# Every fourth weight remainder of a down projection formed by an accumulating DMA within the SBUF

## The chip, the cores and the metric

The kernel runs on one core of one Trainium2 chip. The metric is the device time in microseconds (us) of one execution.

## What is computed

One layer of a diffusion backbone over 256 latent tokens of width 2048: a mixer (gated DeltaNet heads beside a convolution branch, with 256 context tokens) and then a SwiGLU feed-forward part. The change touches only the last product of the feed-forward part, the one with `w_down` (5632 x 2048, f32):

```python
def swiglu(h, w_gate, w_up, w_down):
    return (jax.nn.silu(h @ w_gate) * (h @ w_up)) @ w_down
...
hf = modulate(rms_norm(x, ffn_norm_pre[i]), sh2, sc2)
x = x + g2 * rms_norm(swiglu(hf, w_gate[i], w_up[i], w_down[i]), ffn_norm_post[i])
```

## The kernel before

**Products in three parts.** Each f32 operand is split into a value rounded to fp32r (`_hi`) and a remainder (`_lo` = f32 value minus `_hi`), and a product is the sum of three TensorE matmuls: hi by hi, hi by lo, lo by hi (`product` in the TensorE program, L1848).

**Units.** A weight is streamed in units of 128 partitions x 1024 f32 (512 KB). A unit passes through three tiles of four slots each (`RING = 4`, L47): SyncE loads it from HBM to `raw`; ScalarE copies `raw` to `w_hi` with rounding (L968, from `split`, L1295); VectorE subtracts, `w_lo = raw - w_hi` (L1376, from `split`, L1373); TensorE then runs 12 matmuls of 512 columns on it (two halves of 512 columns of the unit, two tiles of 128 tokens, three parts; `unit`, L2188). The gate and up projections take NG = 176 units, the down projection ND = 88 (v = 0 to 87, the loops at L793, L1325, L1799, L2229 and L2249).

**What orders the work.** Each engine runs its own program in order and waits on semaphores. For unit v of the down projection:

- SyncE issues the load of unit v into `raw` when both `w_hi` and `w_lo` of unit v - 4 have been written from the same slot (L795 and L796). It takes the units in order, so a wait for one unit also holds the loads of all later ones.
- ScalarE starts `w_hi` of unit v when the load has landed and when TensorE has finished unit v - 4, which frees the slots of `w_hi` and `w_lo` (L1296 and L1297). So a unit can be split at the earliest three units of TensorE time ahead of its use.
- VectorE forms `w_lo` when `w_hi` is there.
- TensorE waits for both semaphores `S["hi"]` and `S["lo"]`, which count units.

**Beside it.** From v = 8 to v = 54 two of every three units are accompanied by one 512 KB block of `w_mod` (32 in all, for the output gate): SyncE loads it to one of the four slots of `gin` behind the load of unit v + 1 (L807 to L812), and VectorE adds it to `macc` (L1816) behind the remainder of unit v. GpSimd's last work in the kernel is the load of `x` to `x1` before the feed-forward part (L963). At the end come the squares, the norm and eight stores of 256 KB (L1833 to L1840, L816).

**The last units.** The last four units are run token tile by token tile (L2249), and then the output is normed and stored.

The loop of SyncE:

```python
for v in range(ND):
    U = NG + v
    sp.wait_ge(S["hi"], B0 + U - RING + 1)
    sp.wait_ge(S["lo"], B0 + U - RING + 1)
    cc, g = divmod(v, FT // 2)
    sp.dma_start(raw[:, (R0 + U) % RING, :].rearrange("p (a b) -> p a b", a=2),
```

Of the kernel before, what the change touches and what calls it, by code (L numbers as in the profile page):

```python
# [21 lines left out]
F32 = mybir.dt.float32  # L22
F32R = mybir.dt.float32r
I32 = mybir.dt.int32
ALU = mybir.AluOpType
# [444 lines left out]
def layer(nc, x, cond, ctx, c_ctx, w_mod, b_mod, mix_norm_pre, mix_norm_post, w_in, qkv_conv, a_log, dt_bias,  # L470
# [9 lines left out]
    with es:  # L480
# [128 lines left out]
        def sem(name):  # L609
# [12 lines left out]
        f_mm, f_sg, f_an, f_tr, f_ah, f_al, f_sq, f_yg, f_rt, f_rc, f_out, f_end = (  # L622
            sem(f"f_{n}") for n in ("mm", "sg", "an", "tr", "ah", "al", "sq", "yg", "rt", "rc", "out", "end"))

        def need(eng, kind, *key):
            eng.wait_ge(S[kind], COUNT[kind, key])

# [106 lines left out]
        ND = 4 * (FT // 2)  # L734
        NG2 = 2 * KT
        GATE_AT = {8 + 3 * k // 2: k for k in range(NG2)}


        seq_h = {CTX: (hc_hi, hc_lo), LAT: (h_hi, h_lo), FFN: (h_hi, h_lo)}
# [4 lines left out]
        def _(sp):  # L744
# [48 lines left out]
            for v in range(ND):  # L793
                U = NG + v
                sp.wait_ge(S["hi"], B0 + U - RING + 1)  # L795
                sp.wait_ge(S["lo"], B0 + U - RING + 1)  # L796
                cc, g = divmod(v, FT // 2)
                sp.dma_start(raw[:, (R0 + U) % RING, :].rearrange("p (a b) -> p a b", a=2),
                             w_down_v[:, 2 * g:2 * g + 2, 512 * cc:512 * (cc + 1)]).then_inc(
                    landed[(R0 + U) % RING], 16)  # L800
                if v == 6:
                    need(sp, "yg", 1, 3)
                    sp.dma_start(gw_all[:, :], ffn_norm_post[0].partition_broadcast(P)).then_inc(small_in["c"], 16)
                    sp.wait_ge(S["zero"], 2)
                    sp.dma_start(macc[0:1, :], b_mod[0:1, 5 * D:6 * D]).then_inc(small_in["c"], 16)
                    sp.wait_ge(f_mm, NG)
                if v - 1 in GATE_AT:  # L807
                    k = GATE_AT[v - 1]
                    if k >= 4:
                        sp.wait_ge(g_acc, A0 + k - 3)  # L810
                    sp.dma_start(gin[:, k % 4, :],
                                 w_mod_v[:, k // 2, 5 * D + UN * (k % 2):5 * D + UN * (k % 2 + 1)]).then_inc(mod_in[k % 4], 16)  # L812
# [8 lines left out]
        def _(pool):  # L821
# [39 lines left out]
            for kind, key in PLAN:  # L861
# [46 lines left out]
                elif kind == "mk":  # L908
                    s, p, l = key
                    if l == 0:  # L910
                        need(pool, "kc", s, p)
                        need(pool, "lvl")
                    elif l == 1:
                        need(pool, "yone", s, p)
                    else:
                        need(pool, "z", s, p, l - 1)
                    pool.tensor_tensor(mkl[:, :, :, :].rearrange("p t h c -> p (t h) c"),  # L917
                                       kc[:, :, :, :].bitcast(F32).rearrange("p t h c -> p (t h) c"), bc(lvl[:, l, :], 1, 4),
                                       ALU.mult).then_inc(S[kind], 1)
                elif kind == "mlo":  # L920
                    s, p, t = key
                    need(pool, "z", s, p, LEVELS - 1)
                    need(pool, "mhi", s, p, t)
                    pool.tensor_tensor(mlo[:, t, :, :], mn[:, t, :, :], mhi[:, t, :, :].bitcast(F32),
                                       ALU.subtract).then_inc(S[kind], 1)
                elif kind == "vb":

                    s, p, i = key
                    par = PAIRS.index((s, p)) % 2
                    need(pool, "natc", "v", s, p)  # L930
                    need(pool, "bsig", s)
                    if (s, p, i) != (CTX, 0, 0):
                        prev = (s, p, i - 1) if i else (*PAIRS[PAIRS.index((s, p)) - 1], 1)
                        need(pool, "vn", *prev)
                        if i == 0 and prev[0] == LAT:
                            need(pool, "oT", prev[1])
                    for d in range(2):
                        ins = pool.tensor_tensor(rb[:, 2 * d:2 * d + 2, :], kvq["v"][:, par, tile_of(d, i), :, :],
                                                 bc(gates_[s]["beta"][:, d, tile_of(d, i), 2 * p:2 * p + 2], 2, P),
                                                 ALU.mult)  # L940
                    ins.then_inc(S[kind], 1)
                elif kind == "kd":

                    s, p, i = key
                    par = PAIRS.index((s, p)) % 2
                    need(pool, "kn", s, "k", p)
                    need(pool, "eall", s)
                    k = PAIRS.index((s, p))
                    if i:
                        need(pool, "st", s, p, 0)  # L950
                    elif k and PAIRS[k - 1][0] == CTX:
                        need(pool, "st", *PAIRS[k - 1], 1)
                    elif k:
                        need(pool, "mix_hi", p - 1)
                        need(pool, "mix_lo", p - 1)
                    for d in range(2):
                        ins = pool.tensor_tensor(kd[:, 2 * d:2 * d + 2, :], kvq["k"][:, par, tile_of(d, i), :, :],
                                                 bc(ex[s][:, 1, d, tile_of(d, i), 2 * p:2 * p + 2], 2, P), ALU.mult)
                    ins.then_inc(S[kind], 1)
                elif kind == "s2":  # L960

                    need(pool, "mix_lo", NP - 1)
                    pool.dma_start(x1[:, :, :], x_v).then_inc(x_again, 16)  # L963

        @block.scalar
        def _(act):
# [328 lines left out]
            def split(n, land, mm_done):  # L1295
                act.wait_ge(landed[(R0 + n) % RING], land)  # L1296
                act.wait_ge(f_mm, mm_done)  # L1297
                copy(w_hi[:, (B0 + n) % RING, :], raw[:, (R0 + n) % RING, :], "hi")
# [26 lines left out]
            for v in range(ND):  # L1325
                n = R0 + NG + v
                split(NG + v, 16 * (n // RING + 1), NG + v - RING + 1)
                if v == 4:
                    turned_hi(slice(4 * (FC - 1), 4 * FC), FC)
                if v == 8:  # L1330
# [16 lines left out]
        def _(dve):  # L1347
# [449 lines left out]
            with dve.Fori(2, FC) as c:  # L1797
                gate_up(c, False)
            for v in range(ND):  # L1799
                split(NG + v, B0 + NG + v + 1)  # L1800
                if v == 1:
                    product(FC, True)
                if v == 4:
# [40 lines left out]
        def _(pe):  # L1844
# [340 lines left out]
                    if t == NT - 1:  # L2185
                        ins.then_inc(f_mm, 1)

            def unit(slot, ready, k0, left, banks, first, last):  # L2188

                pe.wait_ge(S["hi"], ready)  # L2190
                pe.wait_ge(S["lo"], ready)
                for k in range(2):
                    col = slice(512 * k, 512 * (k + 1))
                    for t in range(NT):
# [34 lines left out]
            for v in range(ND - RING):  # L2229
# [4 lines left out]
                if v == 20:  # L2234
                    pe.wait_ge(f_al, 2 * FC)
                unit((B0 + NG + v) % RING, B0 + NG + v + 1, 2 * g, (act_hi, act_lo), 2 * cc, g == 0,
                     g == FT // 2 - 1)
                if v == 2:
                    turn(FC, True)
                if v in (57, 60):  # L2240
# [6 lines left out]
            for t in range(NT):  # L2247
                tok = slice(P * t, P * (t + 1))
                for v in range(ND - RING, ND):  # L2249
                    slot, k0 = (B0 + NG + v) % RING, 2 * (v % (FT // 2))  # L2250
                    if t == 0:
                        pe.wait_ge(S["hi"], B0 + NG + v + 1)
                        pe.wait_ge(S["lo"], B0 + NG + v + 1)
                    for k in range(2):
                        col = slice(512 * k, 512 * (k + 1))
                        ins = product(PS[:, 6 + t, :], (act_hi[:, k0 + k, tok], act_lo[:, k0 + k, tok]),
# [24 lines left out]
```

## Time and profile before

| | |
|---|---|
| median of 2 runs | 1625.05 us (1623.65 to 1626.45) |
| span of the profiled execution | 1622.9 us |
| TensorE busy | 1538.2 us, 95% of the span |
| VectorE busy | 1043.9 us, 64% |
| ScalarE busy | 769.2 us, 47% |
| GpSimd busy | 227.5 us, 14% |
| read from HBM | 331.15 MB, 205 GB/s over the span |

The profile is one execution on the chip; times in it are us unless marked ns. PE is TensorE, PEld its weight loads, DVE is VectorE, ACT is ScalarE, POOL is GpSimd, SP is SyncE. An engine with a "q" (SPq) is its queue of instructions, where the issues of DMAs appear. Lines (L1376) are lines of the kernel before. Matmuls are pipelined: their records overlap, so that the time of one matmul in a full stream is the distance between starts and not its duration.

### The profile page before, as it was taken

How to read it: one execution, taken by the hardware profiler on the slowest of the kernel's cores; microseconds unless marked ns; L12 is line 12 of the kernel's file. 1: busy time of each engine (PE TensorE's matmuls, PEld its weight loads, DVE VectorE, ACT ScalarE, POOL GpSimd, SP SyncE). 2: the span in 40 equal slices, each digit the busy share in tenths (PEclk: the TensorE clock that was granted, in tenths of full speed). 3: DMA queues.
4: the chain of work that ended last, by engine and by line, in shares of the span. 5: the costliest groups of instructions: out<-in, count | busy, mean ns of one | idle time of the engine just before them, and what ended most of it. 6: DMA issues, size and time to landing. Idle time of an engine off the chain costs nothing.

```text
span 1622.9 us, 25136 instructions
## 1 busy us (share of the span) xinstructions
PE 1538.2 (95%) x9297; PEld 1292.8 (80%) x9297; DVE 1043.9 (64%) x1458; ACT 769.2 (47%) x1045; POOL 227.5 (14%) x236
## 2 busy tenths in 40 slices
PE   4887999998999999999999999999999999999998
PEld 0557788887888898898877888888888888888786
DVE  1436899999896857675577544545454445777554
ACT  5536634444355745467356544444444443443432
POOL 2000223333332333244200000000000000000000
PEclk9998999999999999999999999999999999999999
DMA  9993555655564556554464666666666665998653
GB/s 353 400 378 108 180 186 194 197 178 184 173 202 134 174 199 191 174 196 134 139 231 132 207 185 192 188 188 191 185 192 194 184 191 187 334 325 319 223 187 135
DMA packets 190979, 334.59 MB, mean 206 GB/s; under 512 B 14707, under 2 KB 80355, under 8 KB 189986
## 3 DMA queue, kind: packets, MB, share of 16 engines
q1 hardware_dynamic: 190194, 330.89, 62.8%
q0 software_dynamic: 688, 2.39, 0.5%
q8 instruction: 63, 1.03, 0.2%
q14 instruction: 34, 0.27, 0.0%
HBM read 331.15 MB, written 2.10 MB: 205 GB/s over the span
## 4 chain that ended last, share of the span: by engine, by line
PE 81%; DVE 10%; DMA 2%; SPq 2%; ACT 2%; issue 2%; POOL 0%; DVEq 0%; ACTq 0%; POOLq 0%
PE PS L1848 66%; DVE cacc L1706 3%; DVE w_lo L1409 3%; DMA first<-in_w_mod_dram 2%; PE PS L1854 2%; PE PS L2117 2%; PE PS L2069 2%; PE PS L2163 2%; SPq L755 2%; DVE sil L1534 1%; PE PS L2015 1%; PE PS L1944 1%; PE PS L2059 1%; DVE xyi L1597 1%; DVE gh L1592 1%
## 5 line engine op out<-in xcount | busy, mean ns | idle before, releaser
L968 ACT ACTIVATE w_hi<-raw 128x1024 fp32r<-128x1024 f32 (+1 forms) x422 | 443.9, 1056 | 508.1 <-PE PS L1848 415.5
L1376 DVE TENSOR_TENSOR w_lo<-raw,w_hi 128x1024 fp32r<-128x1024 f32 x264 | 323.0, 1225 | 309.6 <-ACT w_hi L968 309.6
L1848 PE MATMUL PS<-w_hi,h_hi 128*128 128x512 f32 x704 | 275.7, 392 | 0.0
L1848 PE MATMUL PS<-w_hi,h_lo 128*128 128x512 f32 x704 | 274.6, 390 | 0.0
L1848 PE MATMUL PS<-w_lo,h_hi 128*128 128x512 f32 x704 | 274.4, 390 | 0.0
L1848 PE MATMUL PS<-h_hi,w_hi 128*128 128x256 f32 (+1 forms) x784 | 237.4, 303 | 0.0
L1409 DVE TENSOR_TENSOR w_lo<-raw,w_hi 128x1024 fp32r<-128x1024 f32 (+1 forms) x158 | 195.5, 1249 | 57.6 <-ACT w_hi L968 57.6
L1848 PE MATMUL PS<-h_hi,w_lo 128*128 128x256 f32 (+1 forms) x784 | 221.8, 283 | 0.0
L1848 PE MATMUL PS<-h_lo,w_hi 128*128 128x256 f32 (+1 forms) x784 | 221.6, 283 | 0.0
L1848 PEld LDWEIGHTS PS<-h_hi,w_hi 128*128 128x128 f32 (+1 forms) x784 | 148.5, 189 | 36.8 <-issue 30.2
L1848 PEld LDWEIGHTS PS<-w_hi,h_lo 128*128 128x128 f32 x704 | 132.4, 188 | 27.7
L1848 PEld LDWEIGHTS PS<-w_lo,h_hi 128*128 128x128 f32 x704 | 132.5, 188 | 27.1
L1848 PEld LDWEIGHTS PS<-w_hi,h_hi 128*128 128x128 f32 x704 | 132.5, 188 | 27.1 <-issue 0.2
L1848 PEld LDWEIGHTS PS<-h_lo,w_hi 128*128 128x128 f32 (+1 forms) x784 | 148.7, 190 | 0.7
L1848 PEld LDWEIGHTS PS<-h_hi,w_lo 128*128 128x128 f32 (+1 forms) x784 | 148.2, 189 | 0.1
L1848 PE MATMUL PS<-w_hi,act_hi 128*128 128x512 f32 x352 | 137.9, 392 | 0.0
L1848 PE MATMUL PS<-w_hi,act_lo 128*128 128x512 f32 x352 | 137.0, 389 | 0.0
L1848 PE MATMUL PS<-w_lo,act_hi 128*128 128x512 f32 x352 | 136.9, 389 | 0.0
L1706 DVE SCALAR_TENSOR_TENSOR cacc<-ub,vcol,cacc 128x196 f32<-128x196 f32 (+14 forms) x240 | 124.0, 576 | 0.2
L917 POOL TENSOR_TENSOR mkl<-kc,lvl 128x512 fp32r<-128x512 f32 x56 | 82.8, 1479 | 142.1 <-PE PS L2059 108.0
L1848 PE MATMUL PS<-hc_hi,w_hi 128*128 128x256 f32 (+1 forms) x272 | 82.5, 303 | 11.4 <-ACT w_hi L968 4.3
L1534 DVE SCALAR_TENSOR_TENSOR sil<-PS,vcol,sil 128x254 f32<-128x254 f32 (+1 forms) x160 | 76.7, 481 | 16.0 <-ACT sil L1095 10.1
(342 smaller groups left out, 2352.8 us busy)
## 6 DMA issues: line engine op xcount, KB each, us to landing
raw<-in_w_in_dram SPq DMA_DIRECT2D x128, 512.0 KB, 3.9
raw<-in_w_mod_dram SPq DMA_DIRECT2D x96, 512.0 KB, 4.9
raw<-in_w_gate_dram SPq DMA_DIRECT2D x88, 512.0 KB, 3.7
raw<-in_w_up_dram SPq DMA_DIRECT2D x88, 512.0 KB, 3.7
raw<-in_w_down_dram SPq DMA_DIRECT2D x88, 512.0 KB, 4.5
first<-in_w_mod_dram SPq DMA_DIRECT2D x64, 512.0 KB, 9.7
raw<-in_w_out_dram SPq DMA_DIRECT2D x32, 512.0 KB, 4.3
gin<-in_w_mod_dram SPq DMA_DIRECT2D x32, 512.0 KB, 5.9
```

The costliest lines, as they stand in the source:

```text
L755: sp.dma_start(first[:, slot, :].rearrange("p (a b) -> p a b", a=2), w_mod_v[:, 2 * j:2 * j + 2, part * D + q * 512:part * D + (q + 1) * 5 ...
L917: pool.tensor_tensor(mkl[:, :, :, :].rearrange("p t h c -> p (t h) c"), kc[:, :, :, :].bitcast(F32).rearrange("p t h c -> p (t h) c"), bc( ...
L968: act.activation(out_ap, in_ap, ACT.Copy).then_inc(S[kind], 1)
L1376: dve.tensor_tensor(w_lo[:, slot, :], raw[:, (R0 + n) % RING, :], w_hi[:, slot, :].bitcast(F32), ALU.subtract).then_inc(S["lo"], 1)
L1409: dve.tensor_tensor(lo, raw[:, at_ring[u] % RING, 0:sz], hi.bitcast(F32), ALU.subtract).then_inc(done, 1)
L1534: ins = dve.scalar_tensor_tensor(out=o, in0=pr[:, T * h + a + off:T * h + b + off], scalar=vcol[:, col:col + 1], in1=o, op0=ALU.mult, op1= ...
L1706: ins = dve.scalar_tensor_tensor(out=dst, in0=src, scalar=vcol[:, col:col + 1], in1=dst, op0=ALU.mult, op1=ALU.add)
L1848: ins = pe.matmul(out_ap, a[i], b[j], start=start and n == 0, stop=stop and n == 2, skip_group_check=grouped)
L1854: ins = pe.transpose(PS[:, bank_, P * n:P * (n + 1)], src, ident[:, :])
L2069: ins = pe.matmul(PS[:, b, P * n:P * (n + 1)], a, m, start=False, stop=True, skip_group_check=True)
L2117: ins = pe.matmul(PS[:, b, P * n:P * (n + 1)], a, m, start=True, stop=True)
L2163: ins = pe.matmul(PS[32 * tile:32 * tile + 1, 3, :], csil[:, LAT, j:j + 1], raw[:, n % RING, 512 * h:512 * (h + 1)], start=j == 0, stop=j ...
```

## The change

In the down projection the units v = 2, 6, 10, ..., 78 (`BY_DMA`, 20 units, all in the same slot of `raw` and `w_lo`) get their remainder in another way. ScalarE, after it has copied `raw` to `w_hi`, writes minus the same rounded value to `w_lo` (a second copy with scale -1). GpSimd waits for it and issues a DMA from `raw` to `w_lo`, both in the SBUF, that adds to what stands in `w_lo`: raw - w_hi. VectorE leaves these 20 units out. TensorE, and SyncE where it is to load the next unit into the slot of `raw`, wait for the DMA's semaphore in place of VectorE's; the counts of VectorE's semaphore go down by the units left out. The two semaphores are ones that the kernel already has (`S["masks"]` and that of the loads with "dt").

```diff
--- before.py
+++ after.py
@@ -622,6 +622,16 @@
         f_mm, f_sg, f_an, f_tr, f_ah, f_al, f_sq, f_yg, f_rt, f_rc, f_out, f_end = (
             sem(f"f_{n}") for n in ("mm", "sg", "an", "tr", "ah", "al", "sq", "yg", "rt", "rc", "out", "end"))
 
+        f_neg, f_sum = S["masks"], small_in["dt"]
+        NEG0, SUM0 = TOTALS["masks"], 16 * 3
+
+        def rest_ready(eng, v):
+
+            if v in BY_DMA:
+                eng.wait_ge(f_sum, SUM0 + 16 * (BY_DMA.index(v) + 1))
+            else:
+                eng.wait_ge(S["lo"], B0 + NG + v + 1 - sum(u < v for u in BY_DMA))
+
         def need(eng, kind, *key):
             eng.wait_ge(S[kind], COUNT[kind, key])
 
@@ -734,6 +744,7 @@
         ND = 4 * (FT // 2)
         NG2 = 2 * KT
         GATE_AT = {8 + 3 * k // 2: k for k in range(NG2)}
+        BY_DMA = [v for v in range(ND - 2 * RING) if v % 4 == 2]
 
 
         seq_h = {CTX: (hc_hi, hc_lo), LAT: (h_hi, h_lo), FFN: (h_hi, h_lo)}
@@ -793,7 +804,7 @@
             for v in range(ND):
                 U = NG + v
                 sp.wait_ge(S["hi"], B0 + U - RING + 1)
-                sp.wait_ge(S["lo"], B0 + U - RING + 1)
+                rest_ready(sp, v - RING)
                 cc, g = divmod(v, FT // 2)
                 sp.dma_start(raw[:, (R0 + U) % RING, :].rearrange("p (a b) -> p a b", a=2),
                              w_down_v[:, 2 * g:2 * g + 2, 512 * cc:512 * (cc + 1)]).then_inc(
@@ -961,6 +972,10 @@
 
                     need(pool, "mix_lo", NP - 1)
                     pool.dma_start(x1[:, :, :], x_v).then_inc(x_again, 16)
+            for n, v in enumerate(BY_DMA):
+                pool.wait_ge(f_neg, NEG0 + n + 1)
+                pool.dma_start(w_lo[:, (B0 + NG + v) % RING, :].bitcast(F32), raw[:, (R0 + NG + v) % RING, :],
+                               accum_op=ALU.add).then_inc(f_sum, 16)
 
         @block.scalar
         def _(act):
@@ -1325,6 +1340,9 @@
             for v in range(ND):
                 n = R0 + NG + v
                 split(NG + v, 16 * (n // RING + 1), NG + v - RING + 1)
+                if v in BY_DMA:
+                    act.activation(w_lo[:, (B0 + NG + v) % RING, :], raw[:, n % RING, :], ACT.Copy,
+                                   scale=-1.0).then_inc(f_neg, 1)
                 if v == 4:
                     turned_hi(slice(4 * (FC - 1), 4 * FC), FC)
                 if v == 8:
@@ -1797,7 +1815,8 @@
             with dve.Fori(2, FC) as c:
                 gate_up(c, False)
             for v in range(ND):
-                split(NG + v, B0 + NG + v + 1)
+                if v not in BY_DMA:
+                    split(NG + v, B0 + NG + v + 1)
                 if v == 1:
                     product(FC, True)
                 if v == 4:
@@ -2185,10 +2204,13 @@
                     if t == NT - 1:
                         ins.then_inc(f_mm, 1)
 
-            def unit(slot, ready, k0, left, banks, first, last):
+            def unit(slot, ready, k0, left, banks, first, last, v=None):
 
                 pe.wait_ge(S["hi"], ready)
-                pe.wait_ge(S["lo"], ready)
+                if v is None:
+                    pe.wait_ge(S["lo"], ready)
+                else:
+                    rest_ready(pe, v)
                 for k in range(2):
                     col = slice(512 * k, 512 * (k + 1))
                     for t in range(NT):
@@ -2234,7 +2256,7 @@
                 if v == 20:
                     pe.wait_ge(f_al, 2 * FC)
                 unit((B0 + NG + v) % RING, B0 + NG + v + 1, 2 * g, (act_hi, act_lo), 2 * cc, g == 0,
-                     g == FT // 2 - 1)
+                     g == FT // 2 - 1, v)
                 if v == 2:
                     turn(FC, True)
                 if v in (57, 60):
@@ -2250,7 +2272,7 @@
                     slot, k0 = (B0 + NG + v) % RING, 2 * (v % (FT // 2))
                     if t == 0:
                         pe.wait_ge(S["hi"], B0 + NG + v + 1)
-                        pe.wait_ge(S["lo"], B0 + NG + v + 1)
+                        rest_ready(pe, v)
                     for k in range(2):
                         col = slice(512 * k, 512 * (k + 1))
                         ins = product(PS[:, 6 + t, :], (act_hi[:, k0 + k, tok], act_lo[:, k0 + k, tok]),
```

## Rows read from the trace of the kernel before

**Rows 1.** Page, chain that ended last: shares of the span, by engine.

```profile
PE 81%; DVE 10%; DMA 2%; SPq 2%; ACT 2%; issue 2%; POOL 0%; DVEq 0%; ACTq 0%; POOLq 0%
```

**Rows 2.** Chain in order of time, 1340 to 1623 us: start, us, what (first and last pieces).

```profile
1344.56 35.41 PE PS L1848 x156
1379.97 0.87 PE PS L1854 x8
1380.84 149.62 PE PS L1848 x660
...
1542.10 73.50 PE PS L1848 x324
...
1618.62 1.32 DVE x L1840 x2
```

**Rows 3.** Waits, 1360 to 1612 us: who waited for whom, us, times, longest.

```profile
ACT w_hi L968 <- PE PS L1848: 139.4, 84, 3.4
DVE w_lo L1376 <- ACT w_hi L968: 79.2, 80, 2.1
...
ACT w_hi L968 <- DMA raw<-in_w_down_dram: 1.7, 2, 1.5
```

**Rows 4.** Timeline of ACT: start, us, operation [idle before <-releaser].

```profile
1381.85 2.96 ACT L968 ACTIVATE w_hi<-raw 128x1024 fp32r<-128x1024 f32 x3
...
1405.44 1.06 ACT L968 ACTIVATE w_hi<-raw 128x1024 fp32r<-128x1024 f32 x1 [1.66 <-PE PS L1848]
1408.16 1.06 ACT L968 ACTIVATE w_hi<-raw 128x1024 fp32r<-128x1024 f32 x1 [1.66 <-PE PS L1848]
```

**Rows 5.** Timeline of DVE, the same stretch.

```profile
1406.53 1.23 DVE L1376 TENSOR_TENSOR w_lo<-raw,w_hi 128x1024 fp32r<-128x1024 f32 x1 [0.30 <-ACT w_hi L968]
1407.67 1.28 DVE L1816 SCALAR_TENSOR_TENSOR macc<-gin,csil,macc 128x1024 f32<-128x1024 f32 x1
```

**Rows 6.** Timeline of SP, the same stretch.

```profile
1405.53 0.46 SPq L811 DMA_DIRECT2D gin<-in_w_mod_dram  x1
1407.83 0.37 SPq L798 DMA_DIRECT2D raw<-in_w_down_dram  x1
1408.25 0.46 SPq L811 DMA_DIRECT2D gin<-in_w_mod_dram  x1
```

**Rows 7.** Line L798, loads of the down units, and stretches of the DMA view.

```profile
DMA to landing us min/median/max: 3.5/4.5/7.6
...
raw<-in_w_down_dram SPq DMA_DIRECT2D x37, 512.0 KB, 5.0
gin<-in_w_mod_dram SPq DMA_DIRECT2D x25, 512.0 KB, 5.8
...
raw<-in_w_down_dram SPq DMA_DIRECT2D x24, 512.0 KB, 3.6
```

**Rows 8.** Windows: us, PE, PEld, DVE, ACT, POOL busy (count), PEclk, DMA share, GB/s.

```profile
20.00:40.00 20.00, 12.36 (x68) 3.15 (x68) 5.46 (x30) 18.41 (x22) 0.00 (x0) 1.00 1.04 409
60.00:80.00 20.00, 18.01 (x148) 11.67 (x148) 8.38 (x18) 8.89 (x14) 0.00 (x0) 1.00 1.06 402
120.00:140.00 20.00, 13.35 (x82) 11.50 (x81) 11.66 (x28) 9.69 (x18) 0.00 (x0) 0.79 0.45 134
...
1400.00:1500.00 100.00, 100.00 (x443) 82.84 (x442) 74.59 (x62) 40.41 (x41) 0.00 (x0) 1.00 0.92 326
1560.00:1600.00 40.00, 40.00 (x178) 33.13 (x177) 19.26 (x17) 16.63 (x19) 0.00 (x0) 1.00 0.60 195
```

**Rows 9.** GpSimd: its last DMA (timeline), and that DMA from issue to landing.

```profile
821.04 0.78 POOL L963 DMA_DIRECT2D x<-in_x_dram x1 [28.41 <-DVE hc_lo L1678]
...
x<-in_x_dram POOLq DMA_DIRECT2D x1, 2048.0 KB, 9.0
```

## The prediction

> **What bounds the kernel now.** I began with the page's chain that ended last: 81% of it is TensorE, 10% VectorE [rows 1]. The chain in order of time says where: from 1344.56 us to the end of the matmuls at 1615.6 it is TensorE alone, matmul behind matmul, and only about 7 us of norm and store behind it [rows 2]. The whole down projection lies in that stretch. The stretch rows agree: TensorE is busy 100.00 of 100 us at a granted clock of 1.00, while VectorE has 74.59 and ScalarE 40.41 [rows 8]. Then I read who waits. TensorE waits for nobody in this stretch; ScalarE waits 139.4 us in 84 waits for TensorE, since it may write a slot only when the unit four back is done, and VectorE waits for ScalarE [rows 3]. So the splits run as early as the slots let them, and the work of VectorE is off the path.
>
> **The clock of the pipeline.** Two successive copies of ScalarE start at 1405.44 and 1408.16 [rows 4]: a unit of TensorE takes 2.72 us (12 matmuls), four units, one turn of the ring, take 10.88. The down projection is 88 x 2.72 = 239 us. A copy starts right when TensorE has done the unit four back, so TensorE wants the unit 3 x 2.72 = 8.16 us after the start of its copy. Today both parts are there after 2.3 us (copy 1405.44, remainder 1406.53 with 1.23 us [rows 4, 5]), some 5.9 us early; the next load into the same slot is issued then (1407.83 [rows 6]), lands 3.6 us later where there are no gate loads and 5.0 where there are [rows 7], and waits 3 to 5 us more for its copy.
>
> **What is removed.** 20 remainders of VectorE at 1.23 us, 24.6 us of busy time [rows 5]. Worth 0: it lies beside TensorE, which waits for none of it [rows 2, 3]. Where a remainder is left out the next `macc` step may start 1.2 us earlier, which nobody waits for either.
>
> **What is added, cheap parts.** 20 copies of ScalarE with scale -1. I take the price of a copy in a row: three took 2.96 us against 1.06 for one, so 0.95 each, 19 us in all [rows 4]. ScalarE is busy 40% of the stretch [rows 8], so its time is hidden too; behind it waits only the copy of the next unit, 2.72 - 2.01 = 0.7 us later, which isn't delayed. GpSimd has nothing else in this stretch (0.00 busy [rows 8]), so its wait holds nobody; its issue took 0.78 us at the last load of x [rows 9], against SyncE's 0.37 [rows 6].
>
> **The DMA itself.** No row shows an accumulating DMA or one inside the SBUF, so I bound X, the time from ScalarE's negated copy to the semaphore. A plain 512 KB load lands in 3.5 us at best [rows 7]. At the rate of a full queue, 402 GB/s [rows 8], its 0.524 MB take 1.30 us, so 2.2 us are fixed. From below: a plain load plus the slower issue, 3.5 + 0.4 = 3.9. From above: GpSimd's own 2048 KB load, four times the bytes in one direction, 9.0 us [rows 9]. I take the value near the lower end, because the size is the same and only the traffic is more: source and old contents are both read, so two streams, 2.2 + 0.4 + 2 x 1.30 = 5.2 us. With three streams in turn (the write apart too) it would be 6.5. The Trainium skill (Collectives: The Full Stack, The bandwidth ceiling) says that an add in the DMA's stream halves the rate, because it takes two source reads; no row here shows that, and by it X would be the same 5.2. The skill's fit for a DMA issued from GpSimd (DMA: Bandwidth & Descriptors, Anatomy of one DMA), about 2.0 us plus the bytes at 436 GB/s, makes 3.2 us for a plain one, below my lower end; its load of 2 MB would take 6.8, where the trace has 9.0 beside other loads. By that fit rival A below would hold.
>
> **For TensorE's own wait:** 1.06 + 0.95 + 5.2 = 7.2 us, under the 8.16 that there are. Taken alone, the remainder is in time, with 1 us in hand.
>
> **For the slot of `raw` it is another sum.** All 20 units use one slot, so the next load into it starts only after the DMA, and the loads behind it on SyncE's queue, of `raw` and of `gin`, are held with it. The turn of this slot is: copy and negated copy 2.0, DMA X, landing L, and 0.3 for three handoffs of about 0.1 each (my allowance, from copy ends and remainder starts some 0.1 apart [rows 4, 5]). It must not be over 10.88. With X = 5.2 there are 3.4 us for L; in the quiet stretch L is 3.6 to 3.7 [rows 7], so the turn takes 11.2, 0.3 too long. Eight turns lie there (v = 2 and 54 to 78): 8 x 0.3 = 3 us.
>
> **In the stretch of the gate loads** the engines are nearly full: 0.92 share, 326 GB/s [rows 8], 62 transfers in 100 us [rows 7], 6.75 per turn. These are 6.75 x 1.30 = 8.8 us of DMA time out of 10.88. The accumulation adds 2.6, 11.4 us, more than a turn already. On top, SyncE's queue is held until the sum has landed, so that it runs dry: nothing moves in the fixed part of the next load, 2.2 us. The turn becomes 8.8 + 2.6 + 2.2 = 13.6, 2.7 too long; the slot's own turn with L = 5.0 would be 12.5, so the DMA time is what binds. Sums of v = 6 to 50 hold loads in this stretch: 12 turns, 12 x 2.7 = 33 us. The Trainium skill (DMA: Bandwidth & Descriptors, Issuing engines are not separate DMA queues) says the same against this change: a DMA of GpSimd runs on the same 16 engines and interleaves with SyncE's. Were the GpSimd queue separate, this stretch would cost only 12 x 1.6 = 19 us.
>
> **Sum.** 3 + 33 = 36 us on the path, nothing taken from it: 1622.9 + 36 = 1659 for the profiled execution. The median of the runs is 2 us above the span, so 1661; I say 1660.
>
> **The rivals.** (A) The DMA is hidden: X at 3.9 or less, running while older loads still fill the engines, so that the dry 2.2 us don't arise. Then DMA time is 8.8 + 1.3 = 10.1 per turn, under 10.88, and the quiet turn is 2.3 + 3.9 + 3.7 = 9.9. Cost 0 to 10 us, 1623 to 1635. For it: the slack of 5.9 us at the unit and 3 to 5 us at the load. Against it: 0.92 share in 12 of 20 turns [rows 8]. The point that decides is X of about 4 us. (B) The forecast, X from 3.9 with the dry time (12.3 per turn, 12 x 1.4 = 17 us, 1642) to 6.5 (14.9, 12 x 4.0 + 8 x 1.6 = 61 us, 1686). (C) The add itself is slow, so that X is 7 to 9 or more. At 9.0 a quiet turn is 15.0 and the other one 8.8 + 6.4 + 2.2 = 17.4: 8 x 4.1 + 12 x 6.5 = 111 us, 1736; by the slot's turn alone (16.3) 98 us, 1723. TensorE then also waits for the sum itself, since 2.0 + 9 is over 8.16. For it: nothing in the trace prices the add. (D) Faster: the freed 24.6 us of VectorE would have to be on the path somewhere. The place would be a `macc` step late for a remainder; but VectorE waits for ScalarE before nearly all of its remainders (80 waits [rows 3]), so I give it next to nothing; its price is below 5 us. (E) TensorE's clock. The waits of TensorE come back each turn, some 2.7 us long. In one window with TensorE busy 13.35 of 20 us the clock is 0.79, between its levels of 2.4 and 1.2 GHz, and in one with 12.36 it is 1.00 [rows 8], so such gaps may but needn't lower it. A unit at 1.2 GHz takes 2.72 us more: 20 of them, 54 us on top, 1714. The Trainium skill (TensorE: Matmul & The Clock Gate, HAM oscillation) warns of this case, matmuls that start slow behind every wait for a DMA.
>
> **How the numbers follow.** A 0.27, B 0.43, C 0.25, D 0.02, E 0.03. 2% (about what a measurement can tell from no change) is 32.5 us, or 1657.5: 1.6 us per turn over all 20. B straddles it: its lower third, 0.13, counts as no change. Faster by over 2%: 0.02 at most. Within: 0.27 + 0.13 = 0.40. Slower: 0.30 + 0.25 + 0.03 = 0.58. The range goes from A's lower end, 1623, to 1730, inside C, which leaves out some 0.15. B's own range is 1642 to 1686.
>
> **What would show it.** GpSimd's 20 DMAs with a median landing near 5.2 us (3.9 for A, 7 and more for C). TensorE with new waits in the down projection: about 2.7 us each, 12 of them, in the stretch of the gate loads, and next to none later. ScalarE waiting for the loads of every fourth unit in place of TensorE. SyncE waiting for the sum before the loads of v = 6, 10, ... A GB/s in the gate stretch that is lower than 326. VectorE 24 us less busy, ScalarE 19 more. I am wrong if X is well off 5.2, or if the loads behind the held one catch up without the dry time.

## The result

The changed kernel takes 1681.76 us (median of 2 runs, 1679.35 to 1684.16) against 1625.05: 1.034 times the time before, 95% interval 1.032 to 1.036, or 57 us slower. Its profiled execution has a span of 1682.4 us against 1622.9. Times here are medians of the fast runs; two far slower ones (8672 us in the run with TensorE's `w_lo` matmuls last, 3097 us in the one with every fifth unit) are left out.

### The profile after

The page, part 1: busy time of each engine. It answers the table of before.

```profile
PE 1557.2 (93%) x9297; PEld 1304.3 (78%) x9297; DVE 1020.0 (61%) x1438; ACT 787.6 (47%) x1065; POOL 244.6 (15%) x256
```

VectorE is relieved by 23.9 us, ScalarE has 18.4 more, and none of the relief is in the time. The chain of the page, part 4, shows what took the place of TensorE's 81% [rows 1]:

```profile
PE 72%; DMA 11%; DVE 9%; ACT 4%; issue 2%; SPq 2%; POOL 0%; DVEq 0%; ACTq 0%; POOLq 0%
PE PS L1867 57%; DMA w_lo<-raw 5%; DMA raw<-in_w_down_dram 3%; DVE w_lo L1427 2%; DVE cacc L1724 2%; DMA first<-in_w_mod_dram 2%; PE PS L1873 2%; PE PS L2088 2%; PE PS L2136 2%; PE PS L2182 2%; ACT w_hi L983 1%; SPq L766 1%; PE PS L2034 1%; DVE sil L1552 1%; PE PS L1963 1%
```

The sum itself and the load of a weight now stand on the path. (The "sum" is from here on the accumulating DMA.) TensorE runs the same 9297 matmuls and is busy 19.0 us longer, 1557.2 against 1538.2, and it waits 41.3 us for sums, as the waits below show; together these are about the 59.5 us that the span grew. Lines of the changed kernel: L977 is the sum's DMA, L1344 the negated copy, L983 the copy to `w_hi`, L1867 a matmul, L809 a load, L631 and L633 the waits for a sum and for VectorE.

Windows of the changed kernel (us, busy time of PE, PEld, DVE, ACT, POOL, clock, DMA share, GB/s); before, TensorE was busy 100.00 of 100 us in the stretch of the gate loads [rows 8]:

```profile
1450.00:1470.00 20.00, 17.01 (x68) 13.35 (x66) 10.75 (x9) 6.33 (x7) 0.84 (x1) 0.91 0.87 272
1470.00:1490.00 20.00, 13.22 (x54) 10.49 (x54) 8.76 (x8) 7.28 (x10) 0.83 (x1) 0.90 0.72 221
...
1590.00:1616.00 26.00, 26.00 (x109) 20.12 (x108) 11.14 (x12) 10.90 (x11) 1.69 (x2) 1.00 0.71 209
1616.00:1640.00 24.00, 24.00 (x108) 19.87 (x107) 11.00 (x11) 11.95 (x15) 1.69 (x2) 1.00 0.83 246
```

Only the stretch with gate loads is damaged. Behind it TensorE is full again, with a sum in every turn there too. The timeline of GpSimd gives the length of the turns (start, us, instruction):

```profile
1387.63 0.86 POOL L977 DMA_DIRECT2D w_lo<-raw  x1 [12.70 <-ACT w_lo L1344]
...
1570.60 0.84 POOL L977 DMA_DIRECT2D w_lo<-raw  x1 [12.62 <-ACT w_lo L1344]
...
1620.52 0.84 POOL L977 DMA_DIRECT2D w_lo<-raw  x1 [10.06 <-ACT w_lo L1344]
1631.45 0.85 POOL L977 DMA_DIRECT2D w_lo<-raw  x1 [10.09 <-ACT w_lo L1344]
```

From v = 6 to v = 54 there are twelve turns in 183.0 us: 15.25 each, 4.4 over the 10.88 of before, 52 us of the 59.5 that the span grew. The last turn shown, in the quiet stretch behind the gate loads, is 10.93.

Why the two differ is in the landing times (the DMA view of the changed kernel, 1400 to 1500 us, and then 1610 to 1650 us: count, size, median us from issue to landing):

```profile
raw<-in_w_down_dram SPq DMA_DIRECT2D x24, 512.0 KB, 7.3
gin<-in_w_mod_dram SPq DMA_DIRECT2D x17, 512.0 KB, 8.1
w_lo<-raw POOLq DMA_DIRECT2D x7, 512.0 KB, 8.1
...
raw<-in_w_down_dram SPq DMA_DIRECT2D x15, 512.0 KB, 5.0
w_lo<-raw POOLq DMA_DIRECT2D x4, 512.0 KB, 4.4
```

The same sum takes 4.4 us in the quiet stretch and 8.1 beside the gate loads; the loads went from 5.0 and 5.8 [rows 7] to 7.3 and 8.1. Who waits for it (waits of the changed kernel, 1360 to 1672 us, and the same for SP):

```profile
DVE macc L1835 <- DMA gin<-in_w_mod_dram: 87.7, 27, 7.3
ACT w_hi L983 <- DMA raw<-in_w_down_dram: 80.1, 30, 7.7
...
PE PS L1867 <- DMA w_lo<-raw: 41.3, 13, 5.3
...
SPq L631 <- DMA w_lo<-raw: 197.9, 20, 12.6
```

And the chain in order of time shows two loops that take turns (start, us, what):

```profile
1418.39 7.29 DMA w_lo<-raw
1425.70 0.02 SPq L631
1425.72 0.03 issue
1425.75 4.47 DMA raw<-in_w_down_dram
1430.21 0.02 issue
1430.24 1.06 ACT w_hi L983
1431.30 0.95 ACT w_lo L1344
1432.25 0.28 issue
1432.54 8.95 DMA w_lo<-raw
1441.49 0.14 issue
1441.62 4.60 PE PS L1867 x12
...
1446.30 1.06 ACT w_hi L983
```

Loop one: sum, load of `raw` that was held for it, two copies, next sum. Loop two: sum, TensorE's unit that waited for it (4.6 us here and not 2.7), two copies, next sum. Both begin with the sum, and both are some 15 to 16 us long when the sum takes 8 to 9.

What such a sum meets is in the DMA view of its own time. During the one of 1403.80 us the queue of the loads moves 1.53 MB beside the sum's 0.52. All of it together flows at some 400 GB/s in the first 3.2 us, with the loads that had been held for the sum before, and at under 130 in the last 2.

### The profile page after: what moved, and what is told of

It is laid out like the page before. It is cut to its first block, busy times and chain, and to the rows that moved or that the text cites. A ratio compares the mean times of both kernels' runs of the same rounds, so it can differ in the third digit from the quotient of the medians.

```text
span 1682.4 us, 25156 instructions
## 1 busy us (share of the span) xinstructions
PE 1557.2 (93%) x9297; PEld 1304.3 (78%) x9297; DVE 1020.0 (61%) x1438; ACT 787.6 (47%) x1065; POOL 244.6 (15%) x256
## 4 chain that ended last, share of the span: by engine, by line
PE 72%; DMA 11%; DVE 9%; ACT 4%; issue 2%; SPq 2%; POOL 0%; DVEq 0%; ACTq 0%; POOLq 0%
PE PS L1867 57%; DMA w_lo<-raw 5%; DMA raw<-in_w_down_dram 3%; DVE w_lo L1427 2%; DVE cacc L1724 2%; DMA first<-in_w_mod_dram 2%; PE PS L1873 2%; PE PS L2088 2%; PE PS L2136 2%; PE PS L2182 2%; ACT w_hi L983 1%; SPq L766 1%; PE PS L2034 1%; DVE sil L1552 1%; PE PS L1963 1%
## 5 line engine op out<-in xcount | busy, mean ns | idle before, releaser
L983 ACT ACTIVATE w_hi<-raw 128x1024 fp32r<-128x1024 f32 (+1 forms) x422 | 443.7, 1056 | 541.6 <-PE PS L1867 376.6
L1394 DVE TENSOR_TENSOR w_lo<-raw,w_hi 128x1024 fp32r<-128x1024 f32 x244 | 298.4, 1225 | 303.1 <-ACT w_hi L983 303.0
L1867 PE MATMUL PS<-w_hi,h_hi 128*128 128x512 f32 x704 | 275.6, 392 | 0.0
L1867 PE MATMUL PS<-w_hi,h_lo 128*128 128x512 f32 x704 | 274.5, 390 | 0.0
L1867 PE MATMUL PS<-w_lo,h_hi 128*128 128x512 f32 x704 | 274.4, 390 | 0.0
L1867 PE MATMUL PS<-h_hi,w_hi 128*128 128x256 f32 (+1 forms) x784 | 237.7, 303 | 0.0
L1867 PE MATMUL PS<-h_hi,w_lo 128*128 128x256 f32 (+1 forms) x784 | 221.9, 283 | 0.0
L1867 PE MATMUL PS<-h_lo,w_hi 128*128 128x256 f32 (+1 forms) x784 | 221.8, 283 | 0.0
L1867 PE MATMUL PS<-w_hi,act_hi 128*128 128x512 f32 x352 | 144.5, 411 | 41.3 <-DMA w_lo<-raw 41.3
L1867 PEld LDWEIGHTS PS<-h_hi,w_hi 128*128 128x128 f32 (+1 forms) x784 | 148.8, 190 | 36.7 <-issue 31.8
L1867 PEld LDWEIGHTS PS<-w_hi,h_lo 128*128 128x128 f32 x704 | 132.4, 188 | 27.8
L1867 PEld LDWEIGHTS PS<-w_hi,h_hi 128*128 128x128 f32 x704 | 132.4, 188 | 27.3 <-issue 0.2
L1867 PEld LDWEIGHTS PS<-w_lo,h_hi 128*128 128x128 f32 x704 | 132.5, 188 | 26.9
L1867 PEld LDWEIGHTS PS<-h_lo,w_hi 128*128 128x128 f32 (+1 forms) x784 | 149.0, 190 | 0.7
L1867 PEld LDWEIGHTS PS<-h_hi,w_lo 128*128 128x128 f32 (+1 forms) x784 | 148.5, 189 | 0.1
L1867 PE MATMUL PS<-w_lo,act_hi 128*128 128x512 f32 x352 | 141.9, 403 | 0.0
L1867 PE MATMUL PS<-w_hi,act_lo 128*128 128x512 f32 x352 | 141.3, 401 | 0.0
L977 POOL DMA_DIRECT2D w_lo<-raw x20 | 17.0, 848 | 802.7 <-ACT w_lo L1344 802.7
L1867 PEld LDWEIGHTS PS<-w_hi,act_hi 128*128 128x128 f32 x352 | 68.8, 196 | 61.3 <-issue 46.9
```

The source lines that it names most:

```text
L977: pool.dma_start(w_lo[:, (B0 + NG + v) % RING, :].bitcast(F32), raw[:, (R0 + NG + v) % RING, :], accum_op=ALU.add).then_inc(f_sum, 16)
L983: act.activation(out_ap, in_ap, ACT.Copy).then_inc(S[kind], 1)
L1394: dve.tensor_tensor(w_lo[:, slot, :], raw[:, (R0 + n) % RING, :], w_hi[:, slot, :].bitcast(F32), ALU.subtract).then_inc(S["lo"], 1)
L1867: ins = pe.matmul(out_ap, a[i], b[j], start=start and n == 0, stop=stop and n == 2, skip_group_check=grouped)
```

## The experiments

Each edit is against the changed kernel unless said. The runs of the kernel before on the same chips lay at 1625.8 to 1626.7 us.

### Where the sum stands

```diff
-        BY_DMA = [v for v in range(ND - 2 * RING) if v % 4 == 2]
+        BY_DMA = [v for v in range(54, ND - 2 * RING) if v % 4 == 2]
```

> Only the seven sums of v = 54 to 78 are left, those behind the gate loads; every other remainder is VectorE's again. Theory (the price of a sum is its sharing of the DMA engines with the gate loads, which makes it land after 7 to 9 us in place of 4.3): hardly any cost, 1625 to 1631 us, the sums land in about 4.3 us. Rival (each sum costs the same wherever it stands, 57 us / 20 = 2.8 us): 7 x 2.8 = 20 us, 1645 us.

Measured 1626.03 us, ratio 1.0004 (0.9994 to 1.0014): seven sums for nothing. They landed in 4.4 us (min/median/max of the line of the sum), and TensorE stayed full, as the window shows:

```profile
DMA to landing us min/median/max: 4.3/4.4/4.5
...
1500.00:1560.00 60.00, 60.00 (x259) 48.31 (x258) 30.15 (x29) 26.88 (x29) 3.47 (x4) 1.00 0.77 239
```

An equal price per sum is refuted. Nor is there a gain: VectorE's work was free.

Then the gate loads were taken away instead:

```diff
-                    if k >= 4:
-                        sp.wait_ge(g_acc, A0 + k - 3)
-                    sp.dma_start(gin[:, k % 4, :],
+                    if k < 4:
+                        sp.dma_start(gin[:, k % 4, :],
...
-                    dve.wait_ge(mod_in[k % 4], 16 * (2 * NMOD // NF + k // 4 + 1))
+                    if k < 4:
+                        dve.wait_ge(mod_in[k % 4], 16 * (2 * NMOD // NF + k // 4 + 1))
```

> The changed kernel with only the first four of the 32 gate loads; the later steps of macc read these four again and wait for no load (so the output gate is wrong). All 20 sums are left. To be held against the kernel before with the same omission. Theory (sharing with the gate loads is the price): the sums land in 4.3 to 5 us, the cost over its control is under 12 us: 1625 to 1637 us. Rival (the slot's turn is too long anyway, or the sum is dear by itself): the cost stays above 30 us, over 1655 us.

The same edit to the kernel before:

> The control: the kernel before with the same omission of 28 gate loads. TensorE waits for nothing in the down projection before, so both theories expect no gain: 1622 to 1626 us.

Measured 1638.70 us and 1625.58 us: the cost of 20 sums falls from 57 to 13.1 us. The theory had said under 12, so it is a near miss. The chain in order of time and the times of the sums tell where most of the 13 are. The sums of v = 6 and 10 still run in the stretch of the four gate loads and the 1 MB load of `gw_all`, and take 8.56 and 7.84 us; their two turns are 16.0 and 14.5 us long, 8.7 us too long together. From the fourth on the turns are 11.15 in the mean (v = 14 to 54), and the chain looks like this:

```profile
1472.19 0.96 ACT w_lo L1343
1473.15 0.28 issue
1473.43 4.48 DMA w_lo<-raw
...
1477.97 4.58 DMA raw<-in_w_down_dram
1482.55 0.02 issue
1482.57 1.06 ACT w_hi L982
```

This is the turn of the slot: sum, load, two copies and the handoffs, 4.5 + 4.6 + 2.0 + 0.3 + 0.1 = 11.4 us as rounded here, where 10.88 would be free.

### What the add costs

```diff
-                pool.dma_start(w_lo[:, (B0 + NG + v) % RING, :].bitcast(F32), raw[:, (R0 + NG + v) % RING, :],
-                               accum_op=ALU.add).then_inc(f_sum, 16)
+                pool.dma_start(w_lo[:, (B0 + NG + v) % RING, :].bitcast(F32), raw[:, (R0 + NG + v) % RING, :]).then_inc(f_sum, 16)
```

> The 20 DMAs of GpSimd copy raw to w_lo without adding, so the remainder of these units is wrong (the weight itself); everything else, waits and issues too, as in the changed kernel. It prices the add. Theory (the add reads two streams, so it takes twice the DMA time of a copy; 1.3 us less per DMA alone and about twice that beside other loads): the copies land about 1.3 us earlier in the quiet stretch (3.0 us) and 2 to 3 us earlier beside the gate loads, 1650 to 1662 us. Rival (the add costs nothing, the transfer and the held queue do): same landing times, 1678 to 1685 us.

Measured 1663.75 us, ratio 1.023 (1.021 to 1.025): just outside what the theory had named, but on its side. The copy lands in 3.0 us in the quiet stretch (1600 to 1640 us) against 4.4 with the add, and in 6.7 beside the gate loads against 8.1. Its DMA view, 1400 to 1500 us and 1600 to 1640 us, behind the line of GpSimd's queue in the changed kernel and in this one (packets, MB, share of 16 engines, 1400 to 1500 us):

```profile
q0 software_dynamic: 899, 3.29, 16.6%
...
q0 software_dynamic: 1008, 3.67, 9.0%
...
w_lo<-raw POOLq DMA_DIRECT2D x8, 512.0 KB, 6.7
...
w_lo<-raw POOLq DMA_DIRECT2D x3, 512.0 KB, 3.0
```

So the add is 1.4 us of the landing and 18 of the 57 us. The other 39 are there with a plain copy: most of the cost is that of one more transfer of this size in this place, not that of the add. The queue lines say what the add costs the DMA engines: 16.6 us for 3.29 MB is 2.65 us per sum, and 9.0 us for 3.67 MB is 1.29 per copy, half as much. The landing time grows by about the same, though 0.3 of its 1.4 us is GpSimd's longer issue (0.84 us against 0.53). The Trainium skill (Collectives: The Full Stack, The bandwidth ceiling) says that an add in the DMA's stream halves the rate, because of its two source reads; these lines agree.

### TensorE, its clock and VectorE

In this one TensorE runs its 8 matmuls with `w_hi` first and waits only then:

```diff
+                elif v in BY_DMA:
...
+                            for n in range(2):
+                                pe.matmul(PS[:, banks + t, :], left[n][:, k0 + k, tok], w_hi[:, slot, col],
+                                          start=first and k == 0 and n == 0, stop=False)
+                    rest_ready(pe, v)
...
+                            ins = pe.matmul(PS[:, banks + t, :], left[0][:, k0 + k, tok], w_lo[:, slot, col],
+                                            start=False, stop=last and k == 1)
```

> The changed kernel, but in the 20 units with a sum TensorE runs the 8 matmuls with w_hi first, then waits for the sum, then runs the 4 with w_lo. TensorE so wants the sum 1.8 us later, and after it only 0.9 us of matmuls stand before the next copy into the slot. Theory (two loops bind in turn, one over TensorE's unit and one over the held load of raw, both 15 to 16 us long with sums of 8.5 us): only the turns bound by TensorE get shorter, down to the other loop, 5 to 10 us in all: 1672 to 1678 us. Rival (TensorE's late unit alone is the loop): 12 x 1.8 = 22 us off, 1660 us or less.

Measured 1681.19 us: nothing gained, less than either had said. ScalarE's waits for `raw` grew from 80.1 to 142.7 us; with loop two shorter, the chain runs through loop one in every turn up to v = 54, and it was as long.

```profile
ACT w_hi L983 <- DMA raw<-in_w_down_dram: 142.7, 46, 8.7
```

The clock of TensorE falls around its waits: 0.93 from 1400 to 1500 us. The unit behind one of them, in the timeline of the changed kernel, starts at full rate and after some 1.5 us goes on at 0.43 us from start to start in place of 0.23, the lower of the two levels (1.2 GHz):

```profile
1458.13 0.40 PE L1867 MATMUL PS<-w_hi,act_hi 128*128 128x512 f32 x1
1458.37 0.39 PE L1867 MATMUL PS<-w_lo,act_hi 128*128 128x512 f32 x1
...
1459.73 0.63 PE L1867 MATMUL PS<-w_hi,act_lo 128*128 128x512 f32 x1
1460.16 0.63 PE L1867 MATMUL PS<-w_hi,act_hi 128*128 128x512 f32 x1
```

So matmuls whose results nobody uses were put into the wait (here 12 for each of 13 units):

```diff
+                    if v in BY_DMA and 6 <= v <= 54:
+                        for n in range(12):
+                            pe.matmul(PS[:, 6 + n % 2, :], left[0][:, k0, 0:P], w_hi[:, slot, 0:512],
+                                      start=True, stop=True)
                     rest_ready(pe, v)
```

> The changed kernel with 12 more matmuls (2.72 us, results not used) before TensorE's wait for the sum in the 13 units v = 6 to 54, so that it is busy where it waited. Rival theory (the granted clock of 0.90 to 0.93 behind the waits costs time by itself): the clock comes back to 1.00 and the time falls by some 12 to 17 us, 1665 to 1670 us. Theory (the loop over the load of raw is as long, so the clock matters little): the clock comes back too, but the time stays within 5 us of the changed kernel, 1677 to 1686 us.

Measured 1681.11 us with a clock of 1.00 from 1400 to 1500 us:

```profile
1400.00:1500.00 100.00, 93.53 (x409) 75.87 (x407) 46.43 (x38) 37.16 (x39) 5.88 (x7) 1.00 0.85 274
```

The clock is back and the time isn't: the chain of this run goes through loop one in every turn from v = 6 to v = 46. So giving the clock back gains nothing that can be measured in the changed kernel, since loop one is as long.

VectorE's 87.7 us of waits for the gate loads were taken away with the traffic left in place:

```diff
-                        sp.wait_ge(g_acc, A0 + k - 3)
+                        sp.wait_ge(mod_in[k % 4], 16 * (2 * NMOD // NF + k // 4))
...
-                    dve.wait_ge(mod_in[k % 4], 16 * (2 * NMOD // NF + k // 4 + 1))
...
-                    dve.scalar_tensor_tensor(out=part, in0=gin[:, k % 4, :], scalar=csil[:, LAT, j:j + 1], in1=part,
+                    dve.scalar_tensor_tensor(out=part, in0=gw_all[:, 0:UN], scalar=csil[:, LAT, j:j + 1], in1=part,
```

> The changed kernel with all gate loads, but the macc steps read gw_all in place of gin and wait for no load (the output gate is wrong). It takes VectorE's waits for the gate loads away (87.7 us in the changed kernel) and leaves the traffic. Theory (the traffic is the price): within 8 us of the changed kernel, 1673 to 1684 us. Rival (remainders are late because VectorE stands behind a late gate load, and SyncE behind those remainders): most of the cost goes, under 1655 us.

Measured 1681.34 us, as the theory had it. VectorE's lateness is a symptom.

### One slot, or SyncE's queue

```diff
-        BY_DMA = [v for v in range(ND - 2 * RING) if v % 4 == 2]
+        BY_DMA = [v for v in range(ND - 2 * RING) if v % 5 == 2]
```

> The changed kernel with a sum in every fifth unit in place of every fourth (v = 2, 7, ..., 77; 16 sums, 10 of them in the stretch of the gate loads), so that successive sums use successive slots and no slot waits for a sum in each turn. Theory (DMA time plus the dry time of the held queue: five units' loads at 1.49 us, 8.44 x 1.49 = 12.6, the sum 2.5, dry 2.6, together 17.7 us against 13.6): 10 x 4.1 = 41 us, 1660 to 1670 us. Rival (the turn of the one slot is what costs): the chain is broken, 1626 to 1645 us.

Measured 1666.10 us (1658.48 to 1670.80), ratio 1.022 (1.019 to 1.025), in the range of the theory. The turns of five units are 17.9 us long (v = 7 to 52) in place of 13.6. Successive sums use different slots here, so it isn't the one slot that carries the delay over. The number fits the theory, but the chain of this run shows another reason than SyncE's queue in most of its turns: loop two with one more unit in it. From 1513.84 us it is the sum, 7.9 us, TensorE's unit that waited and the next one, 7.3, the copies, 2.0, and the handoffs, 0.5, together 17.7. Some turns have a held load behind them as well; how the delay divides between the two is not shown.

### Without the held queue

The source of the sum is here a copy of `raw`, so that SyncE may load the slot again when ScalarE is done:

```diff
-        BY_DMA = [v for v in range(ND - 2 * RING) if v % 4 == 2]
+        BY_DMA = [v for v in range(6, ND - 2 * RING) if v % 4 == 2]
...
-                rest_ready(sp, v - RING)
+                if v - RING in BY_DMA:
+                    sp.wait_ge(f_neg, NEG0 + BY_DMA.index(v - RING) + 1)
+                else:
+                    rest_ready(sp, v - RING)
...
+                    act.activation(anf[:, :, :].rearrange("p a b -> p (a b)"), raw[:, n % RING, :],
+                                   ACT.Copy).then_inc(f_neg, 1)
```

> The sum takes its source from a copy of raw that ScalarE writes to anf (free from v = 6 on; 19 sums), so that SyncE waits for ScalarE and not for the sum. It takes the held queue away and leaves the sums and their traffic, with 0.95 us more of ScalarE ahead of each. Theory (the sum is late because the loads held behind the last sum come in one burst that it has to share the DMA engines with): sums land in about 6 us, TensorE waits little, 1630 to 1645 us. Rival (any sum beside the gate loads takes 8 us, held queue or not): TensorE's loop stays at 3.0 + 0.3 + 8 + 2.7 = 14 us or more, over 1662 us.

Measured 1704.39 us, ratio 1.049 (1.047 to 1.051): slower than the changed kernel by 23 us. The theory missed by 59 us; the rival's open range, over 1662, holds it, though not the rival's sum of 8 us. The DMA view tells why (1400 to 1500 us, then 1610 to 1650):

```profile
w_lo<-anf POOLq DMA_DIRECT2D x6, 512.0 KB, 9.5
...
w_lo<-anf POOLq DMA_DIRECT2D x3, 512.0 KB, 6.5
```

Now the sums are late in the quiet stretch too, 6.5 us against 4.4, though a turn has as many loads. In the changed kernel the held queue keeps loads away from the sum: during the one at 1620.5 us they move 0.39 MB, here during the one at 1634.9 us 0.85 MB. (The source is another tile too; that was not tried apart.) With one more copy and TensorE's unit behind the sum, loop two is 3.0 + 0.3 + 6.5 + 0.1 + 3.0 = 12.9 us even there, and the turns are 12.9 to 13.2. My theory was that without the hold the sum would land sooner, and that fell: less holding made it later. It does not follow that the burst of held loads costs the sum nothing in the changed kernel; the loads of the first 3.2 us of the sum above are that burst.

So loop two was shortened in this kernel, by TensorE's order as above:

> The kernel that lets raw go (sums from a copy in anf) together with TensorE's 4 matmuls with w_lo last, in the 19 units with a sum. In the kernel that lets raw go, 1704 us, the only loop left is over TensorE: 3.0 us of copies, handoffs, the sum, the unit. Theory (that loop sets the time): TensorE's part falls by 1.8 us and by the slow clock in it, 19 turns: 30 to 50 us off, 1655 to 1675 us. Rival (the DMA engines are full and set the time): no change, 1695 to 1707 us.

Measured 1663.52 us, 41 less, as the theory had it. And then ScalarE wrote the two copies for the sum ahead of `w_hi`:

```diff
+                if v in BY_DMA:
+                    act.wait_ge(landed[n % RING], 16 * (n // RING + 1))
+                    act.wait_ge(f_mm, NG + v - RING + 1)
+                    act.activation(w_lo[:, (B0 + NG + v) % RING, :], raw[:, n % RING, :], ACT.Copy, scale=-1.0)
+                    act.activation(anf[:, :, :].rearrange("p a b -> p (a b)"), raw[:, n % RING, :],
+                                   ACT.Copy).then_inc(f_neg, 1)
                 split(NG + v, 16 * (n // RING + 1), NG + v - RING + 1)
```

> As e9, and ScalarE writes the negated copy and the copy in anf before w_hi, so that the sum starts 1.06 us earlier. Theory (loop over TensorE: 1.9 + 0.3 + sum + 0.1 + 0.9 us): in the quiet stretch with sums of 6.5 us it is 9.7, under 10.88, no cost; beside the gate loads with 8.6 us 11.8, then the DMA time (10.1 + 2.5 = 12.6) binds: 12 x 1.8 = 22 us, 1642 to 1655 us. Rival (DMA engines dry or held as in the changed kernel): over 1670 us.

Measured 1635.60 us, ratio 1.0054 (1.0037 to 1.0071), 6 us better than the lower end that the theory gave. Most of the cost is gone, with 19 sums and every gate load in place. The DMA view and the window, 1400 to 1500 us:

```profile
DMA packets 14140, 35.26 MB, mean 353 GB/s; under 512 B 1078, under 2 KB 1078, under 8 KB 14134
q1 hardware_dynamic: 12838, 30.47, 78.6%
q0 software_dynamic: 1296, 4.72, 25.5%
...
w_lo<-anf POOLq DMA_DIRECT2D x9, 512.0 KB, 7.7
...
1400.00:1500.00 100.00, 98.52 (x426) 79.07 (x425) 61.53 (x50) 53.41 (x57) 7.58 (x9) 1.00 1.04 353
```

The bytes moved are 353 GB/s against 326 before [rows 8] and 273 in the changed kernel. So the capacity of the DMA engines was not what bound the changed kernel; it was the length of the loops with a late sum in them. The 12.6 us of DMA time per turn in the expectation are refuted too: the turns here are 11.4 (v = 10 to 50). Here, though, the engines are full, with a share of 1.04, and 11.4 us is just what the prediction had for their work in a turn, 8.8 + 2.6. Loop two of this run has the same length, 2.0 + 0.3 + 7.8 + 0.1 + 1.2 us, so which of the two keeps the turns above 10.88 is not shown; if it is the engines, no order of the copies brings this stretch down to the time before.

The copy that went behind the sum is 1.06 us, 20 us in 19 turns, and the time fell by 28. The sums land in 7.7 us here and took 9.2 in the run before it; why is open.

The clock once more, in the kernel where TensorE's unit stands in the only loop:

> The kernel that lets raw go, with 12 more matmuls (results not used) before TensorE's wait in the 13 units v = 6 to 54. There TensorE's unit stands in the only loop and takes 3.0 to 5.5 us in place of 2.7 after a wait, at a granted clock of 0.89. Theory (in this loop the clock costs its full time): clock back to 1.00, 12 turns x 1.5 us = 15 to 20 us off, 1684 to 1690 us. Rival (the clock costs nothing here either): 1700 to 1706 us.

Measured 1699.79 us, at the rival's edge: 4.6 less than without the filler and not 15 to 20. The clock from 1400 to 1500 us came back only from 0.89 to 0.94, and the intervals of the two ratios, 1.0468 to 1.0506 and 1.0435 to 1.0470, just touch. So this run doesn't settle what the clock costs in that loop.

## Why the prediction was right, and where it was not

The direction and the range (1623 to 1730) held, and so did the own range of the forecast (1642 to 1686). Of the cost I had 36 us where the medians show 57. Step by step:

- **Removed work worth nothing**: shown. VectorE has 23.9 us less, and even the seven sums that cost nothing gained nothing.
- **ScalarE's copies**: 0.95 us each in the chain, 18.4 us in all, hidden, but for their place ahead of the sum. That place counts, since it is part of each loop: moving one copy behind the sum is the only edit between 1664 and 1636.
- **X in the quiet stretch**: 4.4 us against my 5.2, between the bounds. The handoff to GpSimd was 0.28 us and not 0.1. The turn of the slot came out at 10.9 to 11.0 against 11.2, and the seven sums alone there cost 0.3 us, which is within the noise, against my 3 for eight turns. This term was right.
- **The stretch of the gate loads is the step that failed.** I kept X at 5.2 there and then let the DMA time bind, 8.8 + 2.6 + 2.2 = 13.6 us. Measured is X = 8.1, and the turn is 15.25. What gives it is my own formula of the slot's turn with the measured landing times (8.1, and 4.5 for the load that was held): 2.0 + 0.3 + 8.1 + 0.1 + 4.5 = 15.0 us. As bookkeeping my terms of the DMA time were not far off. A sum takes 2.65 us of the engines, and 15% of a turn, 2.3 us, are dry; only a load takes 1.49 us (68.1 us for 23.97 MB) and not 1.30, and with it my sum comes to 6.75 x 1.49 + 2.65 + 2.3 = 15.0 too. But those 1.49 us are no limit of the engines: the run with the sum first passes the same transfers, with no queue held for the sum, in turns of 11.4. So the mechanism named, DMA time that binds, was wrong, and the late sum in two loops takes its place. A landing time of 5.0 against 3.6 us for plain loads [rows 7] had already shown that this stretch stretches every transfer, and I used it for the loads and not for the sum. That the time still fell in the forecast's own range, up to 1686, is in part luck: the forecast stood on an X of 3.9 to 6.5, and here it was 8.1.
- **TensorE's wait for the sum**: I had 7.2 us under 8.16 and so none. With 2.3 + 8.1 = 10.4 it waits 2.2 us or more: 41.3 us in 13 waits. That loop two can then bind alone was not in the forecast; the kernel that lets `raw` go shows it, at 1704 us.
- **SyncE's queue held with the loads behind it**: shown, by 197.9 us in 20 waits and by the held load that stands in loop one; the run with every fifth unit goes mostly through loop two and adds nothing to it. But holding has another side that I had not seen: it shields the sum.
- **The rivals.** A's outcome, no cost, holds for the quiet stretch, with X a little over its 3.9, and fails in the other. C's size of X (7 to 9) came true in the gate stretch, but not for its reason: the add is 1.4 us of it. E's clock did fall, to 0.93 over the gate stretch and to 0.83 in one window of 20 us, and TensorE was busy 19.0 us longer where E had 54; giving the clock back gained nothing measurable here. The Trainium skill (DMA: Bandwidth & Descriptors, Issuing engines are not separate DMA queues) states that DMAs of all issuing engines run on the same 16 engines and interleave; 4.4, 6.5 and 8.1 us for the same sum agree. The Trainium skill's fit (the same page, Anatomy of one DMA), 2.0 us plus the bytes at 436 GB/s, gives 3.2 us; the plain copy's 3.0 us in the quiet stretch agrees, and none of the others does.

What stays open: why a sum beside only the loads of `raw` takes 6.5 us and not some 5.7 (4.4 and one load's passage of 1.3), what the lower clock costs where TensorE's unit is in the only loop, and whether the full engines or loop two set the last 9 us of the run with the sum first.

## What to carry to other kernels

Work moved to a DMA from an engine that nobody waits for gains nothing and gets a latency that depends on what else is in flight: price the DMA at the landing times of the stretch in which it runs, not at its best. Then write down each loop that goes through it, with every copy, handoff and unit of the bound engine in it, and compare the longest with the turn of the ring; where it is too long, shorten what stands around the DMA (issue it first, use its result last), which here took the time from 1704 to 1636 us with the same traffic. Where the engine that was relieved wasn't waited for, the best version of the change is still no faster than the kernel before (1636 us against 1627).

## What the hardware showed that I had not expected

- An accumulating DMA of 512 KB within the SBUF lands in 4.4 us where the queue of loads is held for it and in 5.9 to 6.7 us (medians of three runs) beside the loads of `raw`; beside the gate loads too the medians are 7.7 to 9.5 us. A plain copy in its place lands in 3.0 and 6.7. GpSimd's issue took 0.84 us with the add and 0.53 without.
- With the queue of loads held during the sum it landed 2.1 us sooner in the quiet stretch (4.4 against 6.5).
- The lines of the queues give the time of the DMA engines per transfer of 512 KB: 1.29 us for a plain copy within the SBUF and 2.65 for the sum. A load took 1.49 us in the changed kernel and 1.35 with the sum first, where the engines were fullest. So a time per transfer read where they are not full is no limit: 0.85 of their time went at 273 GB/s in the changed kernel, 1.04 at 353 with the sum first.
